# A two-layer decoder trunk on one core: the probabilities of six attention heads a layer turned by VectorE and a DRAM round trip instead of by TensorE

## The reference

```
h = rms_norm(r, norm_mix_pre)
q_lat, kv_lat, k_pe, dq, dk, dv, g_a, g_b = split(h @ w_in)
# branch A: 8 heads (MLA), 64 + 32 rotary columns for q and k, 64 for v, from normed latents
out_a = causal_attention(qa, ka, va, 1 / sqrt(96)) @ w_o_mla
# branch B: 4 heads, softmax(q1 k1) - lam * softmax(q2 k2), times v of 128 columns, normed per head
out_b = rms_norm(causal_diff_attention(...)) * (1 - lam_init) @ w_o_diff
r = r + rms_norm((sigmoid(g_a) * out_a + sigmoid(g_b) * out_b) @ w_out)
r = r + rms_norm((silu(h2 @ w_gate) * (h2 @ w_up)) @ w_down)      # h2 = rms_norm(r)
```

## Time and profile before

| | |
|---|---|
| runs, us | 801.35, 801.42, 801.6 (median 801.42) |
| the profiled execution, us | 801.93, with a span of 800.1 |
| TensorE clock granted, mean | 0.999 |
| busy | PE 99%, DVE 72%, ACT 57%, POOL 17% of the span |
| DMA | 134.87 MB in all, a mean of 169 GB/s |
| instructions | PE 6300 matmuls, DVE 964, ACT 766, POOL 146 |

### The profile page before, as it was taken

The page is one execution under the profiler, slowest core; times in us unless marked ns, Lnnn a source line. Parts: engine busy times, 40 slices in busy tenths (PEclk is TensorE's granted clock), DMA queues, the critical chain, the costliest instruction groups (busy, mean ns, idle before and its releaser), DMA issues.

```text
span 800.1 us, 16818 instructions
## 1 busy us (share of the span) xinstructions
PE 789.6 (99%) x6300; PEld 765.2 (96%) x6300; DVE 577.6 (72%) x964; ACT 452.9 (57%) x766; POOL 138.7 (17%) x146
## 2 busy tenths in 40 slices
PE   9999999999999999999999999999999999999997
PEld 9999899999999999999999999999899999999885
DVE  6899787497787666766668987875977977676432
ACT  6657655665565444455556567656665754554331
POOL 0212000144421111101122202000443211111000
PEclk9999999999999999999999999999999999999999
DMA  9767433246266555355644674332462665657951
GB/s 334 257 219 237 131 106 106 79 159 199 67 194 215 171 169 177 113 166 173 203 157 138 206 237 137 109 110 96 158 210 76 223 211 182 195 172 196 270 134 52
DMA packets 55531, 134.87 MB, mean 169 GB/s; under 512 B 20896, under 2 KB 21536, under 8 KB 55344
## 3 DMA queue, kind: packets, MB, share of 16 engines
q1 hardware_dynamic: 38608, 131.43, 51.4%
q10 hardware_dynamic: 16864, 2.62, 1.9%
HBM read 131.93 MB, written 2.10 MB: 168 GB/s over the span
## 4 chain that ended last, share of the span: by engine, by line
PE 96%; ACT 2%; DVE 1%; issue 1%; DVEq 0%
PE bank L1316 24%; PE bank L1318 23%; PE bank L1317 23%; PE bank L1350 4%; PE bank L1736 3%; PE bank L1737 3%; PE bank L1738 3%; PE bank L1341 2%; PE bank L1591 2%; PE bank L1560 2%; PE bank L1610 1%; PE bank L1435 1%; PE bank L1409 1%; ACT gates L659 1%; PE bank L1562 1%
## 5 line engine op out<-in xcount | busy, mean ns | idle before, releaser
L869 DVE TENSOR_TENSOR w_lo<-w_raw,w_hi 128x1024 fp32r<-128x1024 f32 x246 | 333.6, 1359 | 37.8 <-ACT w_hi L436 34.9
L1316 PE MATMUL bank<-h_hi,w_hi 128*128 128x272 f32 (+1 forms) x1200 | 346.0, 288 | 0.0
L1318 PE MATMUL bank<-h_hi,w_lo 128*128 128x272 f32 (+1 forms) x1200 | 342.8, 286 | 0.0
L1317 PE MATMUL bank<-h_lo,w_hi 128*128 128x272 f32 (+1 forms) x1200 | 341.9, 285 | 0.0
L436 ACT ACTIVATE w_hi<-w_raw 128x1024 fp32r<-128x1024 f32 x246 | 258.9, 1056 | 120.3 <-PE bank L1318 51.2
L1316 PEld LDWEIGHTS bank<-h_hi,w_hi 128*128 128x128 f32 x1200 | 226.2, 189 | 0.5
L1318 PEld LDWEIGHTS bank<-h_hi,w_lo 128*128 128x128 f32 x1200 | 226.2, 188 | 0.0
L1317 PEld LDWEIGHTS bank<-h_lo,w_hi 128*128 128x128 f32 x1200 | 226.1, 188 | 0.0
L834 POOL TENSOR_TENSOR pbuf<-sbuf,ubuf 128x272 f32<-128x272 f32 (+1 forms) x44 | 38.5, 875 | 205.5 <-DVE ubuf L1246 204.0
L767 POOL TENSOR_TENSOR acc<-acc,sq 128x272 f32<-128x272 f32 (+1 forms) x45 | 47.5, 1056 | 131.9 <-ACT sq L449 131.8
L1246 DVE TENSOR_TENSOR ubuf<-bank,rstd_h 128x272 f32<-128x272 f32 (+1 forms) x44 | 18.9, 431 | 44.8 <-PE bank L1318 44.8
(11 more groups left out here) (238 smaller groups left out, 1218.7 us busy)
## 6 DMA issues: line engine op xcount, KB each, us to landing
w_raw<-weights SPq DMA_DIRECT2D x216, 512.0 KB, 4.0
w_raw<-weights SPq DMA_DIRECT2D x16, 384.0 KB, 3.4
w_raw<-weights SPq DMA_DIRECT2D x16, 320.0 KB, 2.9
w_first<-first_weights SPq DMA_DIRECT2D x2, 512.0 KB, 7.2
x_tok<-x_rows SPq DMA_DIRECT2D x1, 1024.0 KB, 11.0
turn<-y ACTq DMA_DIRECT2D x4, 256.0 KB, 7.1
r_tok<-turn ACTq DMA_DIRECT2D x8, 128.0 KB, 4.3
out_tokens<-o_tok SPq DMA_DIRECT2D x4, 256.0 KB, 2.1
```

What stands on the lines that cost most here:

```text
L869: dve.tensor_tensor(w_lo[:, n % RING, :], w_raw[:, n % RAW, :], w_hi[:, n % RING, :].bitcast(f32), ALU.subtract).then_inc(lo_ready, 1)
L1316: pe.matmul(dst, wh, hi, start=first, stop=False)
L1317: pe.matmul(dst, wh, lo, start=False, stop=False)
L1318: return pe.matmul(dst, wl, hi, start=False, stop=last)
```

## The change

Units 4 to 9 (`MOVED`: six of the eight MLA heads) are no longer transposed on PE. For such a unit:

- DVE takes the reciprocal only; ACT multiplies the exponentials by it (two copies with a scale, `probs`), then DVE turns the 416 columns in blocks of 32 x 32 (`dve.transpose`) into `e_second`, which the units of branch B no longer need.
- SP sends the 32 x 32 blocks to DRAM in four DMAs of 32 partitions x 13 blocks x 32 numbers (`send_probs`), so that in DRAM the matrix lies turned whole; and when all four have landed, fetches it with four more (`fetch_probs`: 256 rows and 128 rows of 128 numbers, and two corners of 16 x 16). The fetch goes into one of four buffers: `pt_a` (two), `pt_b0`, `pt_b1`. The fetch of units 8 and 9 also waits for the product that used the buffer before.
- SP's program becomes, for each of the six: one weight load, four sends, four fetches, next weight load.
- PE's `pv` for a pair of them comes one step later, at u = 7, 9 and 11 instead of 6, 8 and 10, and waits for `probs_landed`. ACT's copy from bank 6 falls away for them, `hi_out` and `out_part` come a step later, and for the pair (8, 9) after the loop.
- POOL clears the four buffers' edges (four memsets a layer) and copies the meta columns into the buffers that are now used.

Three more things are moved: on DVE the spread of the head norm (the transpose into `head_rstd`) comes right behind its reciprocal, ahead of the last two `out_part` and of the `oa` evacuations; ACT's weight splits in the `ob` stage go one slot earlier than its `mix_split`; and the last down projection uses banks 4 to 7 and waits for their early users, not for the last gate/up tile.

The core of the diff:

```diff
+MOVED = range(DIFF_HEADS, UNITS - 2)
...
+def moved_to(l, u):
...
+        (pt_a,), _ = place(base + 4 * ((RAW + 2 * RING) * SLOT + GAIN_COLS + 4 * KC * TOK + 6 * TOK), [("pt_a", [P, 2, N_META + PT_COLS], f32)])
+        (pt_b0,), _ = place(lat_at + 4 * (2 * E_COLS + 2 * (N_META + PT_COLS) + 16 * UNITS), [("pt_b0", [P, N_META + PT_COLS], f32)])
+        assert _ <= lat_at + 4 * 10 * TOK
+        (pt_b1,), _ = place(lat_tmp_at + 4 * TOK, [("pt_b1", [P, N_META + PT_COLS], f32)])
+        moved = nc.dram_tensor("moved", (DEPTH * len(MOVED) * A1, P), f32).ap()
         (pm,), _ = place(lat_tmp_at, [("pm", [16, 3, 256], f32)])
...
+                return pt[:, u % 2, :]
+            return pt_a[:, u % 2, :] if (u - MOVED[0]) // 2 % 2 == 0 else (pt_b0, pt_b1)[u % 2][:, :]
+        def moved_rows(l, u):
...
+                def send_probs(u):
+                    sp.wait_ge(probs_turned, moved_to(l, u))
+                    to = moved_rows(l, u).rearrange("(b k) q -> k b q", k=32)
+                    for g in range(4):
+                        sp.dma_start(to[:, :, 32 * g:32 * g + 32], e_second[32 * g:32 * g + 32, u % 2, :].rearrange("p (b q) -> p b q", q=32)).then_inc(probs_sent, 16)
+                def fetch_probs(u):
+                    if u == MOVED[0]:
+                        sp.wait_ge(edges_padded, l + 1)
+                    if u >= MOVED[0] + 4:
+                        sp.wait_ge(pv_ready, PRODUCTS * l + products_to(u - 4))
+                    if moved_to(l, u) > 1:
+                        sp.wait_ge(probs_landed, 16 * MOVES * (moved_to(l, u) - 1))
+                    sp.wait_ge(probs_sent, 16 * MOVES * moved_to(l, u))
+                    p, rows = probs_of(u), moved_rows(l, u)
+                    sp.dma_start(p[:, N_META + T_B0:].rearrange("p (c q) -> p c q", c=2)[:, :, 0:P], rows[B0:B0 + 2 * P, :].rearrange("(c k) q -> k c q", c=2)).then_inc(probs_landed, 16)
+                    sp.dma_start(p[:, N_META + T_A0:N_META + T_A0 + P], rows[A0:A0 + P, :]).then_inc(probs_landed, 16)
+                    for at, row in ((T_A1, A0 + P), (T_B2, B0 + 2 * P)):
+                        sp.dma_start(p[0:16, N_META + at:N_META + at + 16], rows[row:row + 16, P - 16:]).then_inc(probs_landed, 16)
+                at = plan.slot[l, "gate", 14] + MOVED[0]
...
+                for u in MOVED:
+                    load(at + u - MOVED[0], SLOT)
+                    send_probs(u)
+                    fetch_probs(u)
+                first = at + len(MOVED)
...
                                scale=gain[:, l, G_Q + i:G_Q + i + 1]).then_inc(lat_ready_hi, 1)
@@ -588,6 +656,8 @@
                             act.activation(v_tok[0:n, c, 512 + 256 * (g - 1):768 + 256 * (g - 1)], ps[4 + c][0:n, 0:256], ACT.Copy).then_inc(v_copied, 1)
                 def exps(u):
...
+                        act.wait_ge(probs_turned, moved_to(l, u - 2))
                     for m, (bank, e, s) in enumerate(maps_of(u)):
                         act.wait_ge(negmax_ready, MAPS * l + first_map(u) + m + 1)
                         for part, (a, b) in enumerate(((B0, B1), (A0, A1))):
+                def probs(u):
+                    act.wait_ge(exp_ready, MAPS * l + first_map(u) + 1)
+                    act.wait_ge(sums_inverse, moved_to(l, u))
+                    e, s = maps_of(u)[0][1], sm[u % 2]
+                    act.activation(e[:, B0:B1], e[:, B0:B1], ACT.Copy, scale=s[:, 0:1])
+                    act.activation(e[:, A0:A1], e[:, A0:A1], ACT.Copy, scale=s[:, 1:2]).then_inc(probs_ready, 1)
...
                 def pt_evac(u):
-                    act.wait_ge(pt_ready, UNITS * l + u + 1)
+                    if u in MOVED:
+                        return
+                    act.wait_ge(pt_ready, turned_to(l, u))
...
                     exps(u)
                     if u >= 1:
                         pt_evac(u - 1)
-                    if u >= 2:
+                    if u in MOVED:
+                        probs(u)
+                    if 2 <= u < DIFF_HEADS + 2:
                         hi_out(u - 2)
+                    elif u - 3 in MOVED:
+                        hi_out(u - 3)
                     split(S("gate") + i + HI_AHEAD)
...
+                hi_out(MOVED[-1])
                 pt_evac(UNITS - 1)
...
+                split(S("ob") + HI_AHEAD)
                 for i in range(4):
-                    split(S("ob") + i + HI_AHEAD)
+                    if i < 3:
+                        split(S("ob") + i + 1 + HI_AHEAD)
                     mix_split(2 * i)
                     mix_split(2 * i + 1)
...
+                    ins = pool.memset(p[:, N_META + T_A1:].rearrange("p (c q) -> p c q", q=16)[:, ::(T_B2 - T_A1) // 16, :], 0.0)
+                ins.then_inc(edges_padded, 1)
+                if l == 0:
                     for u in range(UNITS):
-                        if u >= 2:
-                            pool.wait_ge(pv_ready, products_to(u - 2))
-                        pool.tensor_copy(pt[:, u % 2, 0:N_META], ptm[:, u, :]).then_inc(meta_placed, 1)
...
+                    if u in MOVED:
+                        dve.reciprocal(s[:, 0:2], s[:, 0:2]).then_inc(sums_inverse, 1)
+                        dve.wait_ge(probs_ready, UNITS * l + u + 1)
+                        if u - 2 in MOVED:
+                            dve.wait_ge(probs_sent, 16 * MOVES * moved_to(l, u - 2))
+                        dve.transpose(e_second[:, u % 2, :], e[:, 0:A1]).then_inc(probs_turned, 1)
+                        return
...
                     probs(u)
-                    if u >= 2:
-                        out_part(u - 2)
+                    if u - 3 in MOVED:
+                        out_part(u - 3)
                     gate(i)
...
-                out_part(UNITS - 1)
                 K = K0 + NDIFF
                 n = head_blocks(l)
                 dve.wait_ge(norm_std, K + 1)
                 dve.reciprocal(head_rec[:, 0:n], head_std[:, 0:n]).then_inc(norm_rec, 1)
+                dve.wait_ge(norm_rec, K + 1)
+                dve.transpose(head_rstd[:, 0:32 * n].rearrange("p (b j) -> p b j", j=32), head_rec[:, 0:n, None].to_broadcast([P, n, 32])).then_inc(norm_bc, 1)
+                out_part(MOVED[-1])
+                out_part(UNITS - 1)
...
-                    if m == 1:
-
-                        dve.wait_ge(norm_rec, K + 1)
-                        dve.transpose(head_rstd[:, 0:32 * n].rearrange("p (b j) -> p b j", j=32), head_rec[:, 0:n, None].to_broadcast([P, n, 32])).then_inc(norm_bc, 1)
...
@@ -1583,6 +1686,8 @@
                         pe.wait_ge(probs_ready, UNITS * l + u + 1)
                     if u == 0:
                         pe.wait_ge(probs_padded, l + 1)
+                    else:
+                        pe.wait_ge(pt_copied, turned_to(l, u) - 1)
...
                 def pv(u):
-                    pe.wait_ge(pt_copied, UNITS * l + u + 1)
-                    if not ends_product(u):
-                        return
+                    if u in MOVED:
+                        pe.wait_ge(probs_landed, 16 * MOVES * moved_to(l, u))
+                    else:
+                        pe.wait_ge(pt_copied, turned_to(l, u))
...
-                        pe.matmul(ps[7][a:b, first_at:TOK], v_tok[:, 0, col:col + b - a], pt[:, unit % 2, first_at:N_META + T_A1], start=True, stop=False)
+                        pe.matmul(ps[7][a:b, first_at:TOK], v_tok[:, 0, col:col + b - a], probs_of(unit)[:, first_at:N_META + T_A1], start=True, stop=False)
...
@@ -1628,11 +1734,14 @@
                         if u < UNITS - 1:
                             scores(u + 1)
-                        if u:
+                        if 0 < u <= DIFF_HEADS:
                             pv(u - 1)
+                        elif u - 2 in MOVED and ends_product(u - 2):
+                            pv(u - 2)
                         if u == UNITS - 2:
                             head_sums()
-                        transposes(u)
+                        if u not in MOVED:
+                            transposes(u)
...
-            d0, g_last = S("down"), TL("gu") + 2 * FC
...
-                dst = ps[2 * c + n][:, :]
+                dst = ps[4 + 2 * c + n][:, :]
```

42 lines of the change are left out of this document (35 added, 7 removed).

## The result

The change makes the kernel slower: 825.73 us (median of 4 runs, 825.33 to 826.03) against 801.38 us for the kernel before in the same series (4 runs, 801.11 to 801.6), a ratio of 1.0303, 95% interval 1.0291 to 1.0315. The forecast had the sign (slower, 806.6), but 24.3 us is nearly five times the predicted 5.2 and far outside the range. The profiled execution took 825.33 us with a span of 822.9; the mean granted clock was 0.987. In the runs further down a median is that of all executions, and the ratios leave out one execution of `v5_products_later`, which took 1272.93 us at a mean granted clock of 0.557.

The account below looks back on a forecast made before the run. PE, busy 99% of the span, was taken as the bound. A layer: -2.95 (transposes) + 5.0 (DMA waits) + 1.4 (behind the loop) - 0.5 (`ob`) = +2.95; two layers less 0.7: +5.2, 806.6 us, range 796 to 812.

Parts of the forecast that it names:

- When does it land?: SP's round of load, sends, wait and fetches takes 6.0 us against a 4.4 us step; PE waits 5.0 us a layer.
- S: Time on SP from a load's issue to the landing of the sends behind it: taken as 4.6 us, lower bound 3.4.
- the upper bound of S: Sends queue behind the load on SP: 3.5 us for its landing plus 1.5 for their data, 5.0.
- the wait behind the loop: In `oa`, PE waits for DVE's low part of pair (8, 9): 1.4 us a layer, 1.8 without DMA waits.
- the last down projection: At the last down projection the banks are long free: its 0.5 us wait and some refill go, 0.7 us saved.
- the wait at `ob`: Ahead of `ob`, the earlier spread shortens DVE's work: 0.5 us a layer saved of PE's 1.3 us wait.
- ACT's splits at nothing: In `ob`, ACT's splits one slot earlier move nothing on which PE waits: no time.
- the next two products late and the first free: PE's `pv(5)` doesn't wait; `pv(7)`'s fetch is 1.6 us late, `pv(9)`'s lands at 154.1 against 149.1.
- SP keeps pace: Rival: S near 3.4, no DMA wait in the loop, 1.8 us a layer behind it: 797.4 us; chance 0.38.
- just keeps pace: In the loop, DVE's round of 4.35 us fits PE's average step of 4.4, so nothing is charged.
- The 3.8 us from scores to blocks: In the steps, a unit's turned blocks are ready on DVE 3.8 us after its scores are done.
- The dear strided turn: Rival: a strided send through DRAM costs 19 times a plain store, kernel some 1150 us; chance under 0.01.

Follow-up runs that it names:

- v5_products_later: v1 with PE taking the products of the moved units one loop step later, the last amid the `oa` blocks: 802.11 us, ratio 1.0002.
- a3: The change with fetches that read rows of the weights and don't wait for the sends, so probabilities are wrong: 799.76 us, ratio 0.9975.
- b1: The kernel before with only the last down projection moved to banks 4 to 7 and its wait to the banks: 800.72 us, ratio 0.9992.
- b2: The kernel before with only the head norm's spread put directly behind its reciprocal, ahead of `out_part(11)`: 800.61 us, ratio 0.9991.
- b3: The kernel before with only ACT's `ob` weight splits one slot earlier: 801.64 us, ratio 1.0003.
- v1: The change with each fetch behind the next unit's sends and DVE's copy of product (8, 9) ahead of the head norm: 805.95 us, ratio 1.0053.
- v3: v1 with the fetches issued from POOL's queue, as soon as a unit's sends have landed, instead of SP's: 809.22 us, ratio 1.0094.
- a2: The change with a unit's four sends ahead of the weight load on SP, the fetch still waiting for them: 809.72 us, ratio 1.0093.
- c1: The change with one send a unit for the same bytes, not in blocks, so probabilities land in the wrong place: 817.08 us, ratio 1.02.
- a1: The change with each unit's fetch behind the next unit's sends on SP: 808.22 us, ratio 1.0094.

## Why the prediction was right in sign and wrong in size

- **The step that failed is "When does it land?", the sum of SP's round.** It had S = 4.6 and S + 1.4 = 6.0; measured were 5.5 (mean of the first five) and 5.5 + 1.88 = 7.38. The mechanism was right: SP's chain of load, sends, wait and fetches is longer than a step of the loop, and the lag adds up. Two terms of its sum were mis-sized. The *issue*: 0.33 us, the load's, was taken for every DMA; a send takes 0.475 (median of the 24 in layer 0, 0.34 to 0.62) and the fetches 0.38, 0.47 and 0.43 twice, so four sends 1.9 to 2.2 instead of 1.3, and a fetch with its surroundings 1.88 instead of 1.4. And *the upper bound of S* (5.0) wasn't one: all six values lie over it, and the forecast took 4.6, below it. The bound was a load's landing, 3.5, and 1.5 for the data of the sends behind it. In the change a load that is followed by sends lands after 3.8 to 4.0 us, and the last of its sends 1.2 to 2.3 us later still (it is issued 2.0 to 2.1 us after the load and lands in 3.0 to 4.3). So S is made as the bound had it, the sends behind the load in the queue, with both parts too small; the allowance for an overlap, which took 0.4 off, isn't seen. (Only unit 4's S has another cause, the wait for DVE's blocks ahead of its sends.)
- Over five rounds 1.38 us more makes 6.9 (6.5 on the clock, since the first load went 0.3 earlier): unit 9's load goes at 152.81, not 146.3, and with its S of 6.4 the fetch ends PE's wait at 162.26, not 154.1. That is 8.2 us in layer 0. Taken for layer 1 too, which the change lengthens about as much (the first matmul of `ob` comes 11.5 us later in layer 0, and 11.9 more in layer 1), it is 16.3 of the 18.2 by which the profiled execution (825.33) lies over its forecast of 807.1.
- **The rest of the 18.2**: the wait behind the loop came out at 0.25 a layer instead of 1.4, most likely because ACT and DVE catch up while PE waits for DMA (it is 1.35 a layer in a3, where PE hardly waits), so 2.3 less. Against it stands what no term had: behind `pv(9)` the clock is at 0.55 and 0.54 for a window of 3 us in the two layers, by estimate 3 x 0.45 = 1.4 us of work each, 2.7. 16.3 - 2.3 + 2.7 = 16.7; 1.5 us aren't accounted for.
- **Right, and shown by runs of their own**: the last down projection (b1), the wait at `ob` (b2: 0.9 for 1.0), ACT's splits at nothing (b3), the place and size of the wait behind the loop where the blocks are in time (a3: 1.35 a layer for 1.4 to 1.8; v1 shows its cause), the next two products late and the first free in layer 0 (0.7 us late in layer 1). In time b1 and b2 are 0.7 us each, at the edge of what the intervals tell apart; their waits in the profile are clear.
- **The rival "SP keeps pace"** had 797.4; a3 is that case and gave 799.76. It lacked the wait for `e_t` (0.75 a layer), which the kernel before doesn't have. PE reaches the scores of unit 8 sooner by the transposes taken out, and they wait for ACT's exponentials of unit 7. These can't come sooner, since DVE takes the head norm's sum (1.29 us at 128.01 in the change) ahead of unit 7's row maxima (129.22). With 1.5 for it and 0.9 less behind the loop, 798.0 would be expected; 1.8 us of the gain stay unexplained.
- **DVE "just keeps pace" and POOL at nothing** held. DVE's wait for the sends through its two `e_second` buffers was missing from the text and lay under PE's.
- The 3.8 us from scores to blocks and the 3.1 from first fetch to landing (159.19 to 162.26) held.
- **The dear strided turn** was rightly put near nothing: the change's sends of 52 KB land in a median of 3.4 us. Its factor of 19 was set against a plain store of the same size; the page that it names in the Trainium skill (VectorE: DVE Perf Modes, section on the three transpose paths) sets it against the DMA engines' own (xbar) transpose, which no run here uses.
- **The chance** of 0.38 for SP keeping pace was too high: it rested on an S of 3.4 that no row of a small DMA behind a load supported.

## What to carry to other kernels

A queue that sends, waits and fetches in line with its weight loads runs at the sum of its latencies, and any excess of that sum over the step of the loop adds up over the steps: here 7.4 us against 4.4, which made PE wait 9.6 us in layer 0. An error in the sum adds up in the same way: 1.4 us a round became 8 us a layer. Before a DMA is put in such a loop, count its issues one by one, with the time of an issue of that form, and take the landing from the last of them and not from the first. And in this kernel a round trip of about 10 us was hidden by asking for it later (the consumer's order), while another engine to issue it brought 2 us (ACT) or cost 3 (POOL) against v1. Look also at what a shared semaphore makes a DMA wait for: in v5 it was the fetch before.

## What the runs showed of the hardware that was not expected

- An issue on SP takes a time that goes with its form: 0.33 us for a 512 KB load after an idle time, 0.42 between other issues; 0.475 (median) for a block send of 32 x 13 x 32; 0.38 for 256 rows of 128 numbers, 0.47 for 128 rows, 0.42 for a corner of 1 KB. The issue of a 1 KB corner takes as long as that of a 512 KB load.
- The issues of the same fetches take 0.76, 0.56 and 0.5 us on POOL (v3).
- The same four sends land 3.4 us after their first issue ahead of a 512 KB load (a2, unit 6), and 4.75 to 5.8 us directly behind one (the change, units 5 and 6).
- The blocks of 128 bytes weren't dear: one send of 208 KB in rows of 1.7 KB landed in 4.3 us behind the load (c1), and the four block sends of 52 KB in a median of 3.4 each from their own issue. Where the load had gone 2 us ahead (unit 4) it is 2.8 against 2.2 to 2.4.
- After idle times of 3.8 and 5.8 us PE's granted clock goes to 0.50 to 0.55 for some 3 to 6 us *after* it has begun to work again. It can follow a short wait as well: in v5 the idle time was 1.87 us and the next window of 3 us has 0.55, while in a1 the clock stays at 1.00 behind a wait of 2.17. No run here tells which of the two a wait will bring.
